# State space of a hybrid layer: strided recurrences replaced by phase rotation and real scans, by quarters

## The chip, the core and the metric

One core of a Trainium2 chip runs one program. TensorE (PE) multiplies, VectorE (DVE), ScalarE (ACT) and GpSimd (POOL) work on vectors, SyncE (SP) issues transfers. The metric is the device time of one execution in microseconds; the median of three runs is given.

## What is computed

One step of a decoder layer over 2048 prompt tokens and 8 x 8 sample tokens. The part that matters is the S5 state space: 32 groups of 16 channels, each driving 64 complex states, with a constant complex factor a per state:

```python
bu_re = einsum('blgc,gpc->blgp', ug, bb_re); bu_im = einsum('blgc,gpc->blgp', ug, bb_im)
h[t] = a * h[t-1] + bu[t]            # complex, a = exp(lam * dt)
y = einsum('blgp,gcp->blgc', h_re, c_re) - einsum('blgp,gcp->blgc', h_im, c_im)
y = gelu(y + d_skip * u); y = y * sigmoid(y @ w_glu + b_glu)
```

An RWKV-7 head group, an output projection, a ConvFFN and a final norm follow.

## The kernel before

Four functions run one after the other, each with its engines in blocks that all end before the next begins: `project_in` (RMS norm and input projection), `state_space`, `delta_rule` and `dense_tail`. The change is in `state_space` alone. All of it works in f32; a TensorE product of f32 shows as two MATMUL and two LDWEIGHTS instructions, a transpose as one of each.

Tokens are taken in blocks of L = 8, so there are NBL = 256 prompt blocks and 8 sample blocks. Partitions hold 64 states of two groups; j runs over the 16 pairs of groups (`NJ`), and the real and imaginary parts are separate tensors. The order is:

1. u (512 channels x tokens) is turned round by transposes into `U`, in three lots: two of 128 prompt blocks and one of 8 sample blocks (`LOTS`). ScalarE evicts.
2. VectorE makes the parameters: `Ap` (powers 0 to 8 of a), `CA` (C times powers), `R` (B times powers) and `Qp` (powers 8 to 128). TensorE makes the kernel rows K from `CA` and `Bb` (64 products with 64 rows each; `groups` takes groups of one parity into one bank), ScalarE evicts them to `Ks`, and eight transfers place shifted copies into `Tm`, to which VectorE adds d on the diagonal. `R` is transposed to `RT`.
3. The driving term of each block, `RT` x `U`, goes to `H`; ScalarE evicts the real part, VectorE the imaginary.
4. VectorE runs the recurrence over 256 blocks: 15 steps inside each of 16 stretches of 16 blocks (strided views of `H`), 15 steps over the ends (`G`), 16 corrections. Each is `add_product`, eight operations of 256 elements, every one waiting for the last. `h_ready` goes up after half and after all of the corrections.
5. Per lot and group TensorE sums `U` x `Tm` (128 rows), `Hr` x `CAr` and `Hi` x `CAn` (64 rows each, upper or lower half of the array by the parity of the group), ScalarE takes the gelu into `rows`, TensorE transposes back and VectorE copies into u (L2188).
6. The GLU: 96 products over tiles of 352 tokens (L2275), ScalarE's sigmoid, VectorE's product (L2191).

VectorE's operations of a chain are written through the helper `tt` (L2047), which issues one and waits for it.

## Time and profile before

| what | value |
|---|---|
| median of 3 runs | 3719.92 us (3714.68 to 3720.4) |
| profiled execution, its own time | 3721.35 us |
| its span | 3719.6 us |
| mean granted TensorE clock | 0.934 of 2.4 GHz |
| PE busy | 3323.8 us (89%) |
| DVE busy | 2210.6 us (59%) |
| ACT busy | 1165.9 us (31%) |
| POOL busy | 174.8 us (5%) |
| state space, from its first transfer to the next stage's | 482.1 to 920.0 us |

Busy shares are averages over stages that have different limits. An instruction's duration holds its way through the pipeline, so for a dense stream the distance from start to start counts, not the duration. The granted clock is given as a share of 2.4 GHz; 0.50 is 1.2 GHz.

### The profile page before, as it was taken

How to read it: one execution, taken by the hardware profiler on the slowest of the kernel's cores; microseconds unless marked ns; L12 is line 12 of the kernel's file. 1: busy time of each engine (PE TensorE's matmuls, PEld its weight loads, DVE VectorE, ACT ScalarE, POOL GpSimd, SP SyncE). 2: the span in 40 equal slices, each digit the busy share in tenths (PEclk: the TensorE clock that was granted, in tenths of full speed). 3: DMA queues.
4: the chain of work that ended last, by engine and by line, in shares of the span. 5: the costliest groups of instructions: out<-in, count | busy, mean ns of one | idle time of the engine just before them, and what ended most of it. 6: DMA issues, size and time to landing. Idle time of an engine off the chain costs nothing.

```text
span 3719.6 us, 75947 instructions
## 1 busy us (share of the span) xinstructions
PE 3323.8 (89%) x32916; PEld 3146.2 (85%) x32916; DVE 2210.6 (59%) x4339; ACT 1165.9 (31%) x2283; POOL 174.8 (5%) x178
## 2 busy tenths in 40 slices
PE   6899961298899998987889999999999999999997
PEld 6899951175678787877889999999999999999997
DVE  6655568931677777743455555565555655555555
ACT  4333330011444545432332222232222322222432
POOL 0000000000110101001210000000000000000121
PEclk8999975579899999988999999999999999999999
DMA  4443320000100100003332222222222222222222
GB/s 145 132 145 115 112 43 0 0 2 29 30 23 23 32 23 23 18 15 97 96 92 69 68 71 72 69 63 69 71 72 69 63 69 73 70 68 73 82 85 85
DMA packets 332589, 237.73 MB, mean 64 GB/s; under 512 B 16720, under 2 KB 319440, under 8 KB 332240
## 3 DMA queue, kind: packets, MB, share of 16 engines
q1 hardware_dynamic: 332256, 232.87, 21.5%
q8 instruction: 260, 4.26, 0.5%
q14 instruction: 73, 0.60, 0.1%
HBM read 206.28 MB, written 25.38 MB: 62 GB/s over the span
## 4 chain that ended last, share of the span: by engine, by line
PE 47%; DVE 3%; DMA 2%; issue 1%; ACT 1%; SPq 0%; DVEq 0%; ACTq 0%
PE tail_bank L987 27%; PE tail_bank L1024 13%; PE tail_bank L1043 5%; DMA tail_raw<-in_w_out 2%; PE tail_bank L975 2%; PE tail_bank L1056 1%; ACT tail_w_hi L634 1%; DVE tail_x L787 0%; DVE tail_xn_lo L792 0%; DVE tail_xn_lo L775 0%; DVE mix_b L799 0%; DMA tail_raw<-in_w_pg 0%; DVE mix_b L918 0%; DVE mix_a L799 0%; DMA tail_raw<-in_w_gate 0%
## 5 line engine op out<-in xcount | busy, mean ns | idle before, releaser
L987 PE MATMUL tail_bank<-tail_xn_hi,tail_w_hi 128*128 128x352 f32 x2112 | 682.4, 323 | 9.5 <-DVE tail_xn_lo L792 9.5
L987 PE MATMUL tail_bank<-tail_xn_lo,tail_w_hi 128*128 128x352 f32 x2112 | 680.5, 322 | 0.0
L987 PE MATMUL tail_bank<-tail_xn_hi,tail_w_lo 128*128 128x352 f32 x2112 | 680.5, 322 | 0.0
L987 PEld LDWEIGHTS tail_bank<-tail_xn_hi,tail_w_hi 128*128 128x128 f32 x2112 | 397.5, 188 | 13.0 <-issue 7.3
L987 PEld LDWEIGHTS tail_bank<-tail_xn_lo,tail_w_hi 128*128 128x128 f32 x2112 | 397.8, 188 | 0.1
L987 PEld LDWEIGHTS tail_bank<-tail_xn_hi,tail_w_lo 128*128 128x128 f32 x2112 | 397.7, 188 | 0.0
L1024 PE MATMUL tail_bank<-tail_f_hi,tail_wd_hi 128*128 128x352 f32 x1056 | 341.8, 324 | 7.2 <-DVE mix_b L893 2.7
L1024 PE MATMUL tail_bank<-tail_f_lo,tail_wd_hi 128*128 128x352 f32 x1056 | 339.6, 322 | 0.0
L1024 PE MATMUL tail_bank<-tail_f_hi,tail_wd_lo 128*128 128x352 f32 x1056 | 339.6, 322 | 0.0
L770 DVE TENSOR_TENSOR tail_w_lo<-tail_raw,tail_w_hi 128x1024 fp32r<-128x1024 f32 x180 | 220.6, 1226 | 165.6 <-ACT tail_w_hi L634 165.4
L634 ACT CAST tail_w_hi<-tail_raw 128x1024 fp32r<-128x1024 f32 x180 | 185.5, 1046 | 406.4 <-DMA tail_raw<-in_w_gate 210.8
L384 PE MATMUL in_pp<-in_x_hi,in_w_hi 128*128 128x352 f32 x864 | 285.7, 331 | 26.2 <-DVE in_w_lo L266 25.5
L385 PE MATMUL in_pp<-in_x_lo,in_w_hi 128*128 128x352 f32 x864 | 283.2, 328 | 0.0
L386 PE MATMUL in_pp<-in_x_hi,in_w_lo 128*128 128x352 f32 x864 | 282.9, 327 | 0.0
L856 DVE TENSOR_SCALAR tail_cv<-tail_gp,tail_cw 128x352 f32<-128x352 f32 (+1 forms) x132 | 60.7, 460 | 361.2 <-ACT tail_gp L695 184.0
L1024 PEld LDWEIGHTS tail_bank<-tail_f_hi,tail_wd_hi 128*128 128x128 f32 x1056 | 198.3, 188 | 12.9 <-DVE mix_a L893 7.1
L1024 PEld LDWEIGHTS tail_bank<-tail_f_lo,tail_wd_hi 128*128 128x128 f32 x1056 | 198.4, 188 | 0.0
L1024 PEld LDWEIGHTS tail_bank<-tail_f_hi,tail_wd_lo 128*128 128x128 f32 x1056 | 198.3, 188 | 0.0
L384 PEld LDWEIGHTS in_pp<-in_x_hi,in_w_hi 128*128 128x128 f32 x864 | 167.1, 193 | 29.1 <-DVE in_w_lo L266 14.6
L695 ACT COPY tail_gp<-tail_bank 128x352 f32<-128x352 f32 x110 | 50.0, 454 | 440.9 <-PE tail_bank L987 440.9
L2252 PE MATMUL ss_bk<-ss_Tm,ss_U 128*128 128x128 f32 (+1 forms) x192 | 53.2, 366 | 137.4 <-DVEq L2177 137.4
L385 PEld LDWEIGHTS in_pp<-in_x_lo,in_w_hi 128*128 128x128 f32 x864 | 166.9, 193 | 0.6 <-issue 0.5
(441 smaller groups left out, 6952.2 us busy)
## 6 DMA issues: line engine op xcount, KB each, us to landing
tail_raw<-in_w_gate SPq DMA_DIRECT2D x66, 512.0 KB, 4.0
tail_raw<-in_w_val SPq DMA_DIRECT2D x66, 512.0 KB, 4.0
tail_raw<-in_w_down SPq DMA_DIRECT2D x66, 512.0 KB, 3.6
in_raw<-in_w_in SPq DMA_DIRECT2D x54, 512.0 KB, 4.1
in_xs<-in_xT SPq DMA_DIRECT2D x12, 1408.0 KB, 6.8
scratch_zr<-in_zo SPq DMA_DIRECT2D x84, 176.0 KB, 1.9
rw_z<-scratch_zr SPq DMA_DIRECT2D x16, 896.0 KB, 5.6
tail_raw<-in_w_out SPq DMA_DIRECT2D x24, 512.0 KB, 4.6
```

The lines of the kernel that those rows point to most:

```text
L384: pe.matmul(out, wh[:, k, :], xh[:, k, tok(n)], start=(k == 0), stop=False)
L385: pe.matmul(out, wh[:, k, :], xl[:, k, tok(n)], start=False, stop=False)
L386: mm = pe.matmul(out, wl[:, k, :], xh[:, k, tok(n)], start=False, stop=(k == KD - 1))
L634: act.copy(as_block(weight_slot(i)[0], i), raw[i % NRAW][:]).then_inc(w_hi, 1)
L695: act.copy(gp[:, 2 + n * TW:2 + (n + 1) * TW], pg[b][:, 0:TW]).then_inc(gate_out, 1)
L770: dve.tensor_tensor(as_block(lo, i), raw[i % NRAW][:], as_block(hi, i).bitcast(F32), ALU.subtract).then_inc(w_lo, 1)
L856: end = dve.tensor_scalar(out, row(2), tap[2], tap[3], ALU.mult, ALU.add)
L975: mm = pe.matmul(pp[i % NPP][:, 0:TW], l, r, start=(k == 0 and j == 0), stop=(k == KD - 1 and j == 2))
L987: mm = pe.matmul(out[:, 0:TW], l, r, start=(k == 0 and j == 0), stop=(k == KD - 1 and j == 2))
L1024: mm = pe.matmul(pd[i % 4][:, 0:TW], l, r, start=(q == 0 and j == 0), stop=(q == G - 1 and j == 2))
L1043: mm = pe.matmul(eg[i % 3][:, 0:TW], l, r, start=(k == 0 and j == 0), stop=(k == KD - 1 and j == 2))
L2252: pe.matmul(out, U[:, g, b0:b0 + n], Tm[:, g, :], start=True, stop=False)
```

## The change

The states are handled in four quarters of four pairs j (`JC`), one per 128 channels (`ct`), with two sets of `U` and `H` in turn. The recurrence over blocks is done otherwise: with a^8 = rho * e^(i phi), the driving terms are multiplied by e^(-i phi n), after which real and imaginary parts each follow h[n] = rho h[n-1] + b[n] with a real factor. A hardware scan along the 256 blocks does that, and the result is turned back by e^(i phi n). The factors of the turn for blocks 0 to 127 (`turn_low`) are made by GpSimd in seven doublings, those of 128 to 255 (`turn_high`) by VectorE. In each quarter VectorE makes the real part of the turned driving terms and GpSimd the imaginary part (`im_ready`), two products and a difference; the scans and the turning back are VectorE's.

Beside that: u is turned round quarter by quarter (`own_rows`) through two banks, and ScalarE evicts both parts of the driving terms (`driven`) and the transposes back into u (`channels`). The block's tokens are held in reverse slots. `R` and `CA` are each made in six whole operations. d is added by GpSimd to a 16-row `Ks` ahead of the transfers rather than to `Tm` after them. In the K products and in the outputs the two parities alternate from product to product, into two banks; the eight full products of a quarter's lot come first and the sixteen half ones after. The GLU is as before, on other banks.

```diff
-        U = e.sb("U", [P, NG_, NBT])
-        H = [e.sb(n, [P, NJ, NBL + 1]) for n in ("Hr", "Hi")]
+        turn_low, turn_high = (e.sb(n, [P, 2, NJ, HALF_NB]) for n in ("turn_low", "turn_high"))
+        NU, NH = GB_ * NBT, 2 * JC * (NBL + 1)
+        own = [e.sb(f"own{i}", [P, NU + NH]) for i in range(2)]
+        U = [o[:, 0:NU].rearrange("p (g n) -> p g n", g=GB_) for o in own]
+        H = [o[:, NU:].rearrange("p (x j n) -> p x j n", x=2, j=JC) for o in own]
+        T = e.sb("T", [P, 4, JC, NBL])
...
+                sp.wait_ge(k_ready, 1)
+                sp.wait_ge(zero, 6)
                 for s in range(L):
-                    sp.dma_start(Tm[s * GC:(s + 1) * GC, :, s * GC:P], Ks[:, :, 0:P - s * GC]).then_inc(t_moved, 16)
-                sp.wait_ge(end_ready, 2)
...
+                def tt(out, a, b, op):
+                    count[0] += 1
+                    pool.tensor_tensor(out, a, b, op).then_inc(links, 1)
+                    pool.wait_ge(links, count[0])
+                pool.wait_ge(pw_ready, 1)
+                pool.wait_ge(zero, 6)
+                w = 1
+                for i in range(NW - 1):
+                    by = [bcast(x[:, i, :], w) for x in Pw]
+                    first, then = [[turn_low[:, x, :, a:a + w] for x in range(2)] for a in (0, w)]
+                    t = T[:].rearrange("p k j n -> p k (j n)")[:, 0, 0:NJ * w].rearrange("p (j n) -> p j n", n=w)
+                    tt(then[0], first[0], by[0], ALU.mult)
+                    tt(t, first[1], by[1], ALU.mult)
+                    tt(then[0], then[0], t, ALU.subtract)
+                    tt(then[1], first[0], by[1], ALU.mult)
+                    tt(t, first[1], by[0], ALU.mult)
+                    tt(then[1], then[1], t, ALU.add)
+                    w *= 2
+                pool.sem_inc(low_ready, 1)
+                pool.wait_ge(par_in, 16 * NPAR)
+                pool.wait_ge(ca_ready, 1)
+                pool.tensor_tensor(dI, ident[0:GC, 0:GC].unsqueeze(1).to_broadcast([GC, NG_, GC]), bcast(d[0:GC, :], GC), ALU.mult).then_inc(dI_ready, 1)
+                pool.wait_ge(k_out, 2 * KU)
+                pool.wait_ge(dI_ready, 1)
+                pool.tensor_tensor(Ks[:, :, 0:GC], Ks[:, :, 0:GC], dI, ALU.add).then_inc(k_ready, 1)
+                def turned(out, x, part, ct):
+                    for i, turn in enumerate((turn_low, turn_high)):
+                        at_ = slice(i * HALF_NB, (i + 1) * HALF_NB)
+                        count[0] += 1
+                        pool.tensor_tensor(out[:, :, at_], x[:, :, at_], turn[:, part, JC * ct:JC * (ct + 1), :], ALU.mult).then_inc(links, 1)
+                pool.wait_ge(high_ready, 1)
+                for ct in range(KU):
+                    pool.wait_ge(b_out, 2 * JC * (ct + 1))
+                    if ct:
+                        pool.wait_ge(h_ready, ct)
+                    h = [H[ct % 2][:, x, :, 1:] for x in range(2)]
+                    turned(T[:, 2], h[1], 0, ct)
+                    turned(T[:, 3], h[0], 1, ct)
+                    pool.wait_ge(links, count[0])
+                    pool.tensor_tensor(T[:, 2], T[:, 2], T[:, 3], ALU.subtract).then_inc(im_ready, 1)
...
+                def squared(out, a):
+                    tt(s["x1"], a[0], a[1], ALU.subtract)
+                    tt(s["x2"], a[0], a[1], ALU.add)
+                    link(dve.scalar_tensor_tensor(out[1], a[0], 2.0, a[1], ALU.mult, ALU.mult))
+                    tt(out[0], s["x1"], s["x2"], ALU.mult)
...
+                        tt(x, x, s["x2"], ALU.mult)
+                pw = [[x[:, i, :] for x in Pw] for i in range(NW)]
+                squared(pw[1], [s["cos"], s["sin"]])
+                squared(pw[2], pw[1])
+                squared(pw[0], pw[2])
+                unit(pw[0], s["rho"])
+                for i in range(1, NW):
+                    squared(pw[i], pw[i - 1])
+                    if i % 3 == 0:
...
-                tt(CA[0][:], big[0], big[1], ALU.subtract)
-                tt(big[0], at_[0], c_[1], ALU.mult)
-                tt(big[1], at_[1], c_[0], ALU.mult)
-                tt(CA[1][:], big[0], big[1], ALU.add)
-                dve.tensor_scalar(CA[1][:], CA[1][:], -1.0, None, ALU.mult).then_inc(k_ready, 1)
-                for q in range(L):
-                    a = [bcast(x[:, L - 1 - q, :], GC) for x in Ap]
-                    cmul([R[0][:, :, q, :], R[1][:, :, q, :]], a, [x[:] for x in Bb], t4)
-                dve.sem_inc(r_ready, 1)
-                for i in range(2):
-                    link(dve.tensor_copy(Qp[i][:, 1, :], Ap[i][:, L, :]))
...
-                dve.wait_ge(t_moved, 16 * L)
+                tt(CA[0][:], at_[0], c_[0], ALU.mult)
+                tt(big, at_[1], c_[1], ALU.mult)
+                tt(CA[0][:], CA[0][:], big, ALU.subtract)
...
+                dve.wait_ge(low_ready, 1)
...
-                def add_product(x, a, b, t):
...
-                def run(i):
-                    return [x[:, :, 1 + i:1 + i + BI * (BI - 1) + 1:BI] for x in H]
-                a8 = [bcast(x[:, 1, :], BI) for x in Qp]
-                for i in range(1, BI):
-                    add_product(run(i), a8, run(i - 1), t4)
...
-                    add_product([x[:, :, b] for x in G], a128, [x[:, :, b - 1] for x in G], tj)
-                for r in range(BI):
-                    blocks = [x[:, :, 1 + r * BI:1 + (r + 1) * BI] for x in H]
-                    add_product(blocks, [x[:, 1:, :].rearrange("p i j -> p j i") for x in Qp], [bcast(x[:, :, r], BI) for x in G], t4)
-                    if r % (BI // 2) == BI // 2 - 1:
-                        dve.sem_inc(h_ready, 1)
-                a8s = [bcast(x[:, 1, :], NBS) for x in Qp]
-                add_product([x[:] for x in HS], a8s, [x[:] for x in h0], [x[:, :, 0:NBS] for x in tmp])
...
+                def rotate(ct):
+                    h = [H[ct % 2][:, x, :, 1:] for x in range(2)]
+                    t = [T[:, k] for k in range(4)]
+                    def turned(out, x, part):
+                        for i, turn in enumerate((turn_low, turn_high)):
+                            at_ = slice(i * HALF_NB, (i + 1) * HALF_NB)
+                            last = dve.tensor_tensor(out[:, :, at_], x[:, :, at_], turn[:, part, JC * ct:JC * (ct + 1), :], ALU.mult)
+                        link(last)
+                    dve.wait_ge(b_out, 2 * JC * (ct + 1))
+                    turned(t[0], h[0], 0)
+                    turned(t[1], h[1], 1)
+                    tt(t[0], t[0], t[1], ALU.add)
+                    for x in range(2):
+                        if x:
+                            dve.wait_ge(im_ready, ct + 1)
+                        for jj in range(JC):
+                            j = ct * JC + jj
+                            last = dve.tensor_tensor_scan(t[2 * x + 1][:, jj, :], s["rho"][:, j:j + 1].to_broadcast([P, NBL]), t[2 * x][:, jj, :], 0.0,
+                                                          ALU.mult, ALU.add)
+                    link(last)
+                    turned(t[0], t[1], 0)
+                    turned(t[2], t[3], 1)
+                    tt(h[0], t[0], t[2], ALU.subtract)
+                    turned(t[0], t[1], 1)
+                    turned(t[2], t[3], 0)
+                    tt(h[1], t[0], t[2], ALU.add)
+                    for x in range(2):
+                        last = dve.tensor_copy(endp[x][:, JC * ct:JC * (ct + 1)], H[ct % 2][:, x, :, NBL])
+                    last.then_inc(h_ready, 1)
...
+                        j = ct * JC + jj
+                        for x in range(2):
+                            if j:
+                                pe.wait_ge(b_out, 2 * (j - 1) + x + 1)
+                            for h in range(2):
+                                last = pe.matmul(bk_b[x][NS * h:NS * h + NS, 0:NBT], RT[x][:, j, NS * h:NS * h + NS], U[ct % 2][:, 2 * jj + h, :],
+                                                 start=True, stop=True)
+                            last.then_inc(b_mm, 1)
+                def outputs(ct, lot):
+                    b0, n, _ = LOTS[lot]
+                    i0 = upto(ct) + 2 * lot
+                    if i0 >= 4:
+                        pe.wait_ge(y_out, i0 - 2)
+                    out = [[bk_y[(i0 + q) % 4][0:n, k * P:(k + 1) * P] for k in range(JC)] for q in range(2)]
+                    for q in range(2):
+                        for k in range(JC):
+                            pe.matmul(out[q][k], U[ct % 2][:, 2 * k + q, b0:b0 + n], Tm[:, GB_ * ct + 2 * k + q, :], start=(k == 0), stop=False)
+                    last = [None, None]
+                    for x in range(2):
+                        for k in range(JC):
+                            for q in range(2):
+                                h = slice(NS * q, NS * q + NS)
+                                j = ct * JC + k
+                                state = h0[x][h, j, :] if b0 == NBL else H[ct % 2][h, x, k, b0:b0 + n]
+                                last[q] = pe.matmul(out[q][k], state, CA[x][h, j, 1:, :], start=False, stop=(x == 1 and k == JC - 1))
+                    for q in range(2):
+                        last[q].then_inc(y_mm, 1)
...
+                pe.wait_ge(ca_ready, 1)
+                for c in range(KU):
+                    if c >= 2:
+                        pe.wait_ge(k_out, 2 * (c - 1))
+                    last = [None, None]
+                    for k in range(JC):
+                        for n in range(2):
+                            for q in range(2):
+                                j, h = JC * c + k, slice(NS * q, NS * q + NS)
+                                last[q] = pe.matmul(bk_y[(2 * c + q) % 4][0:GC, k * P:(k + 1) * P], Bb[n][h, j, :], CA[n][h, j, 0:L, :],
+                                                    start=(n == 0), stop=(n == 1))
+                    for q in range(2):
...
+                own_rows(1)
+                driven(1)
+                pe.wait_ge(k_out, 2 * KU)
+                pe.wait_ge(t_moved, 16 * L)
+                for ct in range(KU):
+                    pe.wait_ge(h_ready, ct + 1)
+                    outputs(ct, 0)
+                    outputs(ct, 1)
+                    channels(ct, 0)
+                    outputs(ct, 2)
+                    channels(ct, 1)
+                    channels(ct, 2)
+                    if ct + 2 < KU:
+                        own_rows(ct + 2)
+                        driven(ct + 2)
```

## Rows read from the trace of the kernel before

**Rows 1.** Busy us (and instructions) of PE, PEld, DVE, ACT, POOL per stretch; PEclk, DMA share, GB/s.
```profile
482.10:541.90 59.80, 44.83 (x320) 36.94 (x320) 48.44 (x107) 28.70 (x62) 3.60 (x3) 0.67 0.11 31
...
585.30:722.00 136.70, 0.00 (x0) 0.00 (x0) 125.94 (x308) 0.66 (x1) 0.00 (x0) 0.52 0.00 0
722.00:782.30 60.30, 60.02 (x192) 45.59 (x192) 34.82 (x74) 4.38 (x8) 0.00 (x0) 0.50 0.01 3
782.30:788.80 6.50, 6.05 (x33) 6.05 (x34) 4.90 (x6) 0.39 (x1) 0.00 (x0) 0.58 0.00 0
788.80:822.50 33.70, 33.70 (x193) 25.89 (x192) 2.71 (x3) 4.18 (x7) 0.00 (x0) 1.00 0.00 1
822.50:858.60 36.10, 33.72 (x257) 17.15 (x256) 9.24 (x16) 6.57 (x10) 0.00 (x0) 1.00 0.00 1
858.60:919.90 61.30, 58.76 (x192) 37.24 (x192) 9.82 (x7) 13.27 (x24) 0.00 (x0) 0.97 0.00 1
```

**Rows 2.** Waits, 480 to 921 us: us in total, times, longest.
```profile
PE ss_bk L2252 <- DVEq L2177: 137.4, 1, 137.4
```

**Rows 3.** DVE groups by form in the state space: busy us, mean ns, idle before.
```profile
L2047 DVE TENSOR_TENSOR ss_Hr<-ss_Hr,ss_tmp 128x256 f32<-128x256 f32 x62 | 31.2, 504 | 2.1
...
L2047 DVE TENSOR_TENSOR ss_CAr<-ss_Hr,ss_Hi 128x2304 f32<-128x2304 f32 x1 | 2.6, 2557 | 0.0
```

**Rows 4.** Timeline of DVE after sine and cosine: start us, us.
```profile
492.48 0.18 DVE L2047 TENSOR_TENSOR ss_Apr<-ss_mag,ss_cos 128x16 f32<-128x16 f32 x1 [0.44 <-ACT ss_cos L2004]
492.69 0.17 DVE L2047 TENSOR_TENSOR ss_Api<-ss_mag,ss_sin 128x16 f32<-128x16 f32 x1
```

**Rows 5.** DVE groups by form in the delta rule, 925 to 1650 us.
```profile
L1432 DVE TENSOR_TENSOR rw_yt<-rw_yt,rw_bonus_h 128x512 f32<-128x512 f32 x16 | 11.1, 692 | 0.5
...
L1313 DVE TENSOR_TENSOR_SCAN rw_p_L<-rw_seg,rw_p_w 128x256 f32<-128x256 f32 x1 | 0.7, 692 | 0.0
```

**Rows 6.** POOL groups by form, whole span.
```profile
L1267 POOL TENSOR_TENSOR rw_p_t<-rw_p_t,rw_r_k 128x512 f32<-128x512 f32 x16 | 16.6, 1038 | 1.3
...
L1267 POOL TENSOR_TENSOR rw_p_t<-rw_p_t,rw_r_k 128x256 f32<-128x256 f32 x1 | 0.6, 612 | 0.1
```

**Rows 7.** Timeline of DVE and POOL in the delta rule.
```profile
1126.50 1.23 DVE L1313 TENSOR_TENSOR_SCAN rw_p_L<-rw_seg,rw_p_w 128x512 f32<-128x512 f32 x1
1126.60 1.65 POOL L1256 TENSOR_TENSOR rw_rT<-rw_z,rw_p_E 128x256 f32<-128x256 f32 x1 [17.91 <-DVE rw_p_w L1311]
...
1127.64 1.15 DVE L1318 TENSOR_TENSOR rw_p_t<-rw_p_a,rw_kah 128x512 f32<-128x512 f32 x1
```

**Rows 8.** Timeline of PE in the K products, clock 0.50; entries that overlap are merged.
```profile
522.26 0.63 PE L2222 MATMUL ss_bk<-ss_CAn,ss_Bbi 64*16 64x128 f32 x2
522.68 0.63 PE L2222 MATMUL ss_bk<-ss_CAr,ss_Bbr 64*16 64x128 f32 x4
523.09 0.65 PE L2222 MATMUL ss_bk<-ss_CAn,ss_Bbi 64*16 64x128 f32 x4
```

**Rows 9.** Timeline of SP's queue and DVE around the transfers into Tm.
```profile
542.16 13.90 SPq L1968 DMA_DIRECT2D ss_Tm<-ss_Hi  x8
...
558.63 4.42 DVE L2047 TENSOR_TENSOR ss_Hr<-ss_ident,ss_d 128x4096 f32<-128x4096 f32 x1 [9.05 <-DMA ss_Tm<-ss_Hi]
```

**Rows 10.** Timeline of PE in the driving terms, clock 1.00.
```profile
573.32 0.62 PE L2240 MATMUL ss_bk<-ss_U,ss_RTi 128*64 128x264 f32 x4
...
573.77 0.62 PE L2240 MATMUL ss_bk<-ss_U,ss_RTr 128*64 128x264 f32 x4
```

**Rows 11.** Timeline of PE in the outputs of the sample lot, clock 1.00.
```profile
829.27 0.39 PE L2252 MATMUL ss_bk<-ss_Tm,ss_U 128*8 128x128 f32 x2
...
830.11 0.39 PE L2252 MATMUL ss_bk<-ss_Tm,ss_U 128*8 128x128 f32 x2
```

**Rows 12.** ACT groups by form in the state space.
```profile
L1994 ACT COPY ss_rows<-ss_bk 128x512 f32<-128x512 f32 x16 | 8.1, 671 | 0.0
...
L2018 ACT COPY ss_Hr<-ss_bk 128x256 f32<-128x256 f32 x16 | 6.0, 372 | 29.4 <-PE ss_bk L2240 29.4
```

More of the change, by code:

```diff
@@ L1922, in state_space @@
[L1922 to L1925 removed]
+        dI = B[0:GC].rearrange("p x j c -> p (x j) c")
+        big = own[1][:, 0:NJ * (L + 1) * GC].rearrange("p (j t c) -> p j t c", t=L + 1, c=GC)
@@ L1943, in state_space, with u_turn, x_turn, upto @@
         LOTS = [(0, P, 0), (P, P, P * L), (NBL, NBS, SEQ)]
-        NK = NG_ // 4
+        NLOT = len(LOTS)
         NR = 2 * NJ // 4
-        UF, UG = KU * 2, NG_ // 4
-        UL = UF + UG
-        def groups(i):
-            first = 8 * (i // 2) + i % 2
-            return slice(first, first + 7, 2)
+        UT, XT = 4 * NLOT, 2 * NLOT
+        def u_turn(ct, lot, f):
+            return ct * UT + lot * 4 + f + max(ct - 1, 0) * XT
+        def x_turn(ct, lot, half):
+            return (min(ct, KU - 2) + 2) * UT + ct * XT + lot * 2 + half
+        def upto(ct):
+            return 2 * NLOT * ct
+        def halves(x, ct):
+            return [x[:, i, JC * ct:JC * (ct + 1), :] for i in range(2)]
         with nc.Block() as block:
@@ new lines, in _, with powers @@
+                cmul([x[:] for x in Bb], [bcast(s["fr"], GC), bcast(s["fi"], GC)], [Br, Bi], st)
+                n = 1
+                while n < L:
+                    last = [x[:, n:n + 1, :].to_broadcast([P, n, NJ]) for x in Ap]
+                    t = small_t[:, 0:n * NJ].rearrange("p (i j) -> p i j", j=NJ)
+                    cmul([x[:, n + 1:2 * n + 1, :] for x in Ap], [x[:, 1:1 + n, :] for x in Ap], last, t)
+                    n *= 2
+                def powers(first, count_):
+                    return [x[:, first:first + count_, :].rearrange("p t j -> p j t").unsqueeze(3).to_broadcast([P, NJ, count_, GC]) for x in Ap]
@@ new lines, in _ @@
+                tt(big, at_[1], c_[0], ALU.mult)
+                link(dve.scalar_tensor_tensor(CA[1][:], CA[1][:], -1.0, big, ALU.mult, ALU.subtract))
+                link(dve.memset(H[1][:, :, :, 0:1], 0.0))
+                dve.sem_inc(ca_ready, 1)
+                dve.wait_ge(low_ready, 1)
+                dve.wait_ge(r_mm, NR)
+                for j in range(0, NJ, NJ // 2):
+                    js = slice(j, j + NJ // 2)
+                    by = [bcast(x[:, NW - 1, js], HALF_NB) for x in Pw]
+                    t = T[:, 0].rearrange("p j n -> p (j n)").rearrange("p (j n) -> p j n", n=HALF_NB)
+                    cmul([turn_high[:, x, js, :] for x in range(2)], [turn_low[:, x, js, :] for x in range(2)], by, t)
@@ new lines, in channels @@
+                def channels(ct, lot):
+                    _, n, _ = LOTS[lot]
+                    pe.wait_ge(y_out, upto(ct) + 2 * lot + 2)
+                    for half in range(2):
+                        i = x_turn(ct, lot, half)
+                        pe.wait_ge(t_out, i - 1)
+                        for k in range(4):
+                            c = (4 * half + k) * P
+                            last = pe.transpose(bk_t[i % 2][:, k * n:(k + 1) * n], yrow[lot][0:n, c:c + P], ident[0:n, 0:n])
+                        last.then_inc(t_mm, 1)
@@ L2224, in _ @@
+                own_rows(0)
                 pe.wait_ge(r_ready, 1)
```

340 lines of the change are left out of this document (157 added, 183 removed).

## The prediction

> **What bounds the kernel now.** I read the page first, then the busy time by stretches, then the waits inside the state space. The four stages follow one another with a barrier between them, so time saved in one comes off the end as long as the next does not change. The page gives 3719.6 us of span, and the state space holds 482.1 to about 920 of it. The reader is to see three things in [rows 1]. VectorE works alone for 136.7 us (585.3 to 722.0, TensorE 0.00 busy). The output products then take 60.3 us for the first lot and 33.7 us for the second, though both have 192 instructions: the granted clock is 0.50 (1.2 GHz) in one and 1.00 (2.4 GHz) in the other. Last come the third lot and its transposes (36.1 us) and the GLU (61.3 us), which is TensorE's. [Rows 2] names the big wait: TensorE waits 137.4 us for VectorE's recurrence. The diff touches nothing outside `state_space`, so I take 482.1 us ahead of the stage and 2799.7 us behind 919.9 as they are.
>
> **Prices.** VectorE, contiguous f32 pair operations: 512 elements 0.692, 2304 elements 2.557 us [rows 3, 5], so 1.04 ns an element plus 0.16 us; linked small ones start every 0.21 us [rows 4]. So 256 cost 0.43, 1024 cost 1.23, 2048 cost 2.29, each plus 0.03 for the link. A scan of 256 takes 0.692 us [rows 5], about 0.61 in a run of four, since the next starts under the end of the last. GpSimd: 256 elements 0.612, 512 1.038 us [rows 6], so 1.66 ns an element plus 0.19 us.
>
> **The start.** From the first operation after sine and cosine (492.5, [rows 4]) VectorE now does 59 small operations for the powers of the turn (12.4 us), 4 for rho and 15 for `Ap` and f (4.0), `Bb` 6 x 0.46 = 2.8, powers of `Ap` 18 x 0.26 = 4.6, `R` in six whole operations 6 x 2.32 = 13.9, `CA` 6 x 2.59 = 15.5. That ends at 545.9. `turn_high` is 12 x 1.26 = 15.1 more: 561.0 if nothing disturbs it.
>
> GpSimd makes `turn_low` beside that: 42 operations over 6 x (16 + ... + 1024) = 12192 elements, 20.3 us of elements and 42 x 0.27 of fixed cost, some 32 us from 505. Whether it is beside or instead is what [rows 7] shows: a GpSimd product of 256 elements takes 1.65 us where it meets a VectorE scan with two SBUF inputs, against 0.612 alone, and VectorE's next product of 512 elements takes 1.15 instead of 0.692. They take turns. I charge 15 of the 20.3 us to VectorE, since its small operations are mostly fixed cost; the bounds are 0 and 20. So `ca_ready` is at 561 and the turns are whole at 576.
>
> The Trainium skill (SBUF — State Buffer, "Who interferes with whom") says the same as a rule: a VectorE instruction with two SBUF inputs and a GpSimd instruction that reads SBUF exclude each other for the whole instruction. By that rule the whole 20.3 us of doubling and the 5.1 us of each rotation would be added to VectorE's own; the upper bounds here.
>
> The K products, 64 of them: [rows 8] shows how two 64-row products share the array: four entries apart by 0.42 us hold 2 instructions while they are in one half, and 4 each where the halves change (522.68 and 523.09). The new order changes the half at every product, so 64 x 0.213 = 13.7 us at 1.2 GHz: 561 to 574.7. GpSimd adds d to `Ks` (1.5 us with the eviction). The eight copies into `Tm` before ran from 542.16 until VectorE, which waited for them, started at 558.63 [rows 9]: 16.5 us, so 576.2 + 16.5 = 592.7. On SyncE only the stores of the states stand behind them, whose end the GLU covers. On GpSimd the imaginary parts of all quarters are queued behind this addition: a K product later than 576 would hold the first rotation too. The two VectorE operations on `Tm` (4.42 us each, [rows 9] has the first) go.
>
> **One rotation.** VectorE: two turned products (2.8), a sum (1.3), four scans (2.5), four scans for the imaginary part (2.5), four turned products (5.4), two sums (2.6), copies (0.4) = 17.4 us. GpSimd: 4 x 512 + 1024 = 3072 elements = 5.1 us, which by [rows 7] delays VectorE by the same. 22.6 us, between 17.4 (free) and 26 (dearer GpSimd operations); all on VectorE it would be 21.5. Four of them are 90 us. They replace 46 times `add_product`, eight operations each, at up to 504 ns on average for 256 strided elements [rows 3]: 136.7 us in the open and 35 more under the first outputs [rows 1]. The first is ready at 576 + 22.6 = 598.6, 6 us behind `Tm`. GpSimd starts each one only when VectorE has ended the last (they share `T`), so it never works ahead; that costs nothing as long as they take turns anyway.
>
> **TensorE becomes the bound after that.** Before, three products (128, 64 and 64 rows) took 33.7 / 32 = 1.05 us at full clock, 60.3 / 32 = 1.88 at half [rows 1]. Now a lot of a quarter is 8 full products x 0.32 + 0.2 = 2.8 us and 16 half products in pairs. Columns in pairs overlap fully: 64-column products of 264, two to an item, take 0.45 us an item [rows 10], half of 2 x 4 x 264 / 2.4 GHz. For row pairs I take 0.16 us each; bounds 0.107 (loading hidden) and 0.32 (no pairs). So 5.4 us a lot at 2.4 GHz, 10.6 at 1.2. The sample lot takes 0.84 us for three before [rows 11]; in the new order 8 x 0.21 + 16 x 0.107 + 0.2 = 3.6. The transposes back are 4 us a quarter; their copies into u move from VectorE to ScalarE (0.67 each by [rows 12]), as do the imaginary driving terms. Turning u round for the next quarter passes two banks to and fro: 8 copies of 0.67 and 4 smaller ones taken at 0.4 (7 us), and 8 pairs of 0.37 + 0.17 (4.3, [rows 4, 12]), with the waits for one another 16 us. Gelu and copies make 17 us of ScalarE in a quarter, under TensorE's 34.
>
> The clock: dense outputs stayed at 0.50 for 60.3 us and only 32 transposes raised it (0.58 on average in that stretch, 1.00 after) [rows 1]. In the new order transposes come every quarter and pauses are short, so I charge half clock for two lots of the first quarter only.
>
> Quarter 0: 598.6 + 2 x 10.6 + 3.6 + 4 = 627.4; the next u and its products to 643.4. The third rotation needs these and ends at 666, covered. Quarter 1: 18.4 to 661.8; u of quarter 3 to 677.8. Quarter 2 to 696.2; the fourth rotation runs 677.8 to 700.4 and is late by 4. Quarter 3 to 718.8. GLU starts there, not at 858.6: **139.8 us less**. The GLU's 61.3 us stand [rows 1]. Of the profiled execution's 3719.6 us span 3579.8 remain (its own time is 1.8 us more, the median of the runs 0.3 more). I say **3580**.
>
> **The rivals.** (A) *The clock stays at 1.2 GHz through the outputs.* Six more lots at +5.2, three sample lots at +3.6: 42 us, 3622. For it: 60 us of dense products did not raise it. Against: transposes did, within 6.5 us. 17%. (B) *GpSimd is free beside VectorE.* The first rotation ends at 561.0 + 17.4 = 578.4, `Tm` is there at 577.7, so the start is 20 us earlier, and the fourth rotation is covered (4 us): 3556. Against: [rows 7]. 13%. (C) *No row pairs in the outputs,* each half product 0.32: 8 lots x 2.6 + 4 x 1.7 and drains between full and half products: 3610. Against: [rows 8]. 10%. 8-column products alone would be 3 x 0.213 = 0.64 us and take 0.84 [rows 11], so each group pays 0.2 for going from full to half height and back. The Trainium skill (TensorEngine Tiling (Array Packing), "Key Properties") states that changing the tiling mode drains the array; the trace agrees with its 0.2 us. (D) *Slower: GpSimd prices.* If its operations, with their broadcasts, short inner runs and links, cost more than 7.4 ns an element instead of 1.66, the 12192 + 12288 elements add over 140 us and the gain is gone; at 8 ns it is 3735. The dearest row is 1.65 us for 256, 6.4 ns, and most of that is waiting. 2%. (E) That offloading the imaginary part does nothing is in my own sum: 22.6 against 21.5 us a quarter. My forecast has 58%, its own range 3560 to 3600.
>
> **Range and chances.** Low end: B and loading of weights half hidden (0.13 instead of 0.16, some 4 us) on top, a little more for the handing to and fro: 3545. High end: A with 5 us more lock and 10 us dearer rotations, 3635. A change of 0.2%, 7 us, is about what a measurement of this kernel can tell from none; all cases but D are far beyond it. Faster 0.97, same 0.01, slower 0.02.
>
> **What would show it.** Turned products on VectorE at about 1.1 to 1.4 us instead of 0.69 in the first third of each rotation, and GpSimd products over 1.04, show the turns taken; equal to the rows of before, B. `Tm` copies ending some 6 us ahead of the first rotation. A granted clock of 1.00 in quarters 1 to 3, else A. Two instructions of half products in 0.16 us or less each, else C. GLU starting near 719. The forecast is wrong above all if TensorE waits for VectorE in each quarter, or if the handing to and fro of two banks costs far more than 16 us.

## The result and the profile after

The changed kernel takes 3572.62 us (median of four runs, 3572.05 to 3573.4) against 3720.14 for the kernel before beside it: a ratio of 0.9607, 95% interval 0.959 to 0.9624. That is 147.5 us less, where 139.8 was forecast; 3580 was said and 3572.6 came.

The profiled execution took 3572.05 us with a span of 3570.3. Its stages, by the same columns as [rows 1]:

```profile
482.00:582.00 100.00, 33.15 (x280) 24.93 (x280) 86.49 (x140) 25.56 (x59) 60.02 (x50) 0.65 0.10 22
582.00:605.00 23.00, 5.40 (x43) 2.38 (x41) 22.60 (x26) 6.01 (x21) 8.74 (x6) 0.75 0.23 36
605.00:624.00 19.00, 17.34 (x170) 15.34 (x171) 18.76 (x20) 7.34 (x12) 9.37 (x5) 0.85 0.01 1
624.00:641.00 17.00, 14.15 (x84) 8.91 (x83) 3.08 (x6) 9.71 (x29) 0.00 (x0) 0.70 0.00 1
641.00:713.00 72.00, 56.94 (x582) 46.80 (x580) 46.64 (x58) 31.23 (x64) 19.38 (x10) 0.91 0.01 3
713.00:774.00 61.00, 58.77 (x194) 37.34 (x192) 9.74 (x6) 14.78 (x26) 0.00 (x0) 0.97 0.00 1
```

Up to 582 VectorE (third column of busy time) is the bound, as it was before, but the 136.7 us of the recurrence have shrunk to the 23 us of one rotation. From 605 TensorE's own chain sets the pace; it waits for two rotations and, while it turns u, for ScalarE's copies (14.15 of 17.0 us busy between 624 and 641). The GLU (last line) is what it was in [rows 1]; it starts at 713.0 instead of 858.6, which is 145.6 us of the 149.3 by which the span shrank. The other 3.7 lie in stages that the change does not touch. In the runs below the start of the state space alone moves between 479.7 and 483.8 us with the same code ahead of it, so 3.7 is no result.

The waits of the stage (480 to 780 us: in total, times, longest), the answer to [rows 2]:

```profile
PE ss_bk L2349 <- DVE ss_endi L2293: 23.3, 2, 16.3
DVE ss_T L2271 <- ACT ss_HSi L2081: 22.5, 2, 13.9
```

TensorE waits twice for a rotation, 16.3 us for the first and 7.0 for the last, where it waited 137.4. The second line is the reverse: VectorE waits 13.9 and 8.6 us for the driving terms of the third and fourth quarter.

VectorE and GpSimd at the end of the start, then in the first rotation (timeline: start us, us):

```profile
560.06 4.58 DVE L2248 SCALAR_TENSOR_TENSOR ss_CAn<-ss_CAn,ss_own 128x2304 f32<-128x2304 f32 x1
...
582.05 1.72 DVE L2271 TENSOR_TENSOR ss_T<-ss_own,ss_turn_low 128x512 f32<-128x512 f32 x1
...
588.59 3.25 DVE L2141 TENSOR_TENSOR ss_T<-ss_T 128x1024 f32<-128x1024 f32 x1
591.87 4.77 DVE L2283 TENSOR_TENSOR_SCAN ss_T<-ss_rho,ss_T 128x256 f32<-128x256 f32 x8
596.67 0.69 DVE L2271 TENSOR_TENSOR ss_T<-ss_T,ss_turn_low 128x512 f32<-128x512 f32 x1
...
604.65 0.69 DVE L2271 TENSOR_TENSOR ss_T<-ss_own,ss_turn_low 128x512 f32<-128x512 f32 x1
```
```profile
557.68 4.53 POOL L2005 TENSOR_TENSOR ss_turn_low<-ss_turn_low,ss_T 128x1024 f32<-128x1024 f32 x1
...
583.18 1.63 POOL L2036 TENSOR_TENSOR ss_T<-ss_own,ss_turn_high 128x512 f32<-128x512 f32 x1
```

While GpSimd works, VectorE's operation of 2304 elements takes 4.58 us (2.557 in [rows 3]), its 512 elements 1.7 (0.692 in [rows 5]), its 1024 elements 3.25; when GpSimd is done, the same 512 take 0.69. GpSimd's 1.63 for 512 are dearer than the 1.038 of [rows 6] as well. From the first turned product (582.05) to that of the next rotation (604.65) it is 22.6 us.

TensorE in the first outputs, and at full clock in those of the second quarter (x16 is 8 products):

```profile
604.89 3.75 PE L2349 MATMUL ss_bk<-ss_Tm,ss_own 128*128 128x128 f32 x16 [16.29 <-DVE ss_endi L2293]
608.57 2.08 PE L2357 MATMUL ss_bk<-ss_CAr,ss_own 64*128 64x128 f32 x16
610.44 1.15 PE L2357 MATMUL ss_bk<-ss_CAn,ss_own 64*128 64x128 f32 x16
611.53 2.05 PE L2349 MATMUL ss_bk<-ss_Tm,ss_own 128*128 128x128 f32 x16
...
640.47 2.05 PE L2349 MATMUL ss_bk<-ss_Tm,ss_own 128*128 128x128 f32 x16
642.45 1.16 PE L2357 MATMUL ss_bk<-ss_CAr,ss_own 64*128 64x128 f32 x16
643.45 1.06 PE L2357 MATMUL ss_bk<-ss_CAn,ss_own 64*128 64x128 f32 x16
644.43 0.82 PE L2349 MATMUL ss_bk<-ss_Tm,ss_own 128*128 128x128 f32 x5
```

From start to start, eight full products take 1.98 us and eight half ones 1.00: a lot takes 4.0 us. At 1.2 GHz (first two lines) the same are 3.7 and 1.9. The change from one to the other comes at 610.6, 5.7 us into the outputs (the granted clock is 0.50 up to 610.4, 0.70 over 610.4 to 610.8, then 1.00); [rows 1] show 60 us at 0.50 for the same products in another order.

### The profile page after: what moved, and what is told of

Same layout as the page of the kernel before. It is cut to its first block, busy times and chain, and to the rows that moved or that the text cites. A ratio compares the mean times of both kernels' runs of the same rounds, so it can differ in the third digit from the quotient of the medians.

```text
span 3570.3 us, 75777 instructions
## 1 busy us (share of the span) xinstructions
PE 3247.9 (91%) x32916; PEld 3095.3 (87%) x32916; DVE 2139.0 (60%) x4012; ACT 1190.6 (33%) x2339; POOL 268.4 (8%) x245
## 4 chain that ended last, share of the span: by engine, by line
PE 47%; DVE 3%; issue 3%; DMA 3%; ACT 1%; POOL 0%; SPq 0%; DVEq 0%; POOLq 0%; ACTq 0%
PE tail_bank L987 28%; PE tail_bank L1024 13%; PE tail_bank L1043 3%; DMA tail_raw<-in_w_out 2%; PE tail_bank L975 2%; PE tail_bank L1056 1%; ACT tail_w_hi L634 1%; DVE tail_x L787 0%; DVE tail_xn_lo L792 0%; DVE tail_xn_lo L775 0%; DVE mix_b L799 0%; POOL tail_ssum L625 0%; DMA tail_raw<-in_w_pg 0%; DVE mix_a L799 0%; DVE mix_b L918 0%
## 5 line engine op out<-in xcount | busy, mean ns | idle before, releaser
L386 PEld LDWEIGHTS in_pp<-in_x_hi,in_w_lo 128*128 128x128 f32 x864 | 165.9, 192 | 0.0
```

Source lines behind the costliest of these rows:

```text
L386: mm = pe.matmul(out, wl[:, k, :], xh[:, k, tok(n)], start=False, stop=(k == KD - 1))
```

## The experiments

Besides the time, two places of the profile are compared: the end of the first rotation and the start of the GLU, both counted from the moment at which GpSimd's first wait of the stage ends, because the stages ahead shift by some us from run to run. For the changed kernel these are the rows (waits of GpSimd; timeline of TensorE):

```profile
POOL ss_Apr L1995 <- POOLq L125: 481.5, 1, 481.5
```
```profile
713.02 58.75 PE L2421 MATMUL ss_bk<-mix_a,ss_wglu 128*128 128x352 f32 x192
```

So 231.5 for it (713.02 - 481.5); in e1_im_vector the two are 483.8 and 709.22, and 225.4 the difference. The last two columns come from one execution of each kernel, the profiled one, which took 3563.7 us in e7_all, 3558.1 in e9_turn_first and 3647.9 in e4_old_order, 5 to 8 us more than their medians. All of them:

| kernel | median us | ratio to before, 95% | first rotation over | GLU starts |
|---|---|---|---|---|
| changed | 3572.6 | 0.9607 (0.959 to 0.9624) | 123.2 | 231.5 |
| e1_im_vector | 3567.5 | 0.9583 (0.9569 to 0.9597) | 121.1 | 225.4 |
| e2_low_vector | 3571.2 | 0.9594 (0.958 to 0.9608) | 125.1 | 231.2 |
| e3_apart | 3592.6 | 0.9652 (0.9635 to 0.9668) | 123.1 | 249.3 |
| e4_old_order | 3642.8 | 0.9788 (0.9773 to 0.9803) | 123.3 | 308.0 |
| e5_split | 3563.9 | 0.9582 (0.9569 to 0.9595) | 118.0 | 221.2 |
| e6_early | 3566.3 | 0.9588 (0.9575 to 0.9601) | 123.1 | 226.5 |
| e7_all | 3555.4 | 0.9561 (0.9547 to 0.9575) | 117.7 | 218.1 |
| e8_warm | 3550.9 | 0.9541 (0.9528 to 0.9554) | 117.8 | 209.0 |
| e9_turn_first | 3553.4 | 0.9549 (0.9536 to 0.9562) | 117.7 | 216.8 |

The time spent at 1.2 GHz behind a rotation is not the same in each of these executions, though the products and their order are. In the changed kernel, e1_im_vector, e2_low_vector and e5_split it was 5.7, 4.4, 2.9 and 3.5 us in the first quarter and 4.6, 3.0, 3.5 and 3.5 in the fourth (from the first output to the rise of the granted clock). With what the clock does while u is turned, that moves the start of the GLU by 2 to 3 us, so a smaller difference in the last column is no result.

### e1_im_vector: the imaginary part on VectorE

```diff
 # gpsimd
-                    turned(T[:, 2], h[1], 0, ct)
-                    turned(T[:, 3], h[0], 1, ct)
...
-                    pool.tensor_tensor(T[:, 2], T[:, 2], T[:, 3], ALU.subtract).then_inc(im_ready, 1)
 # vector
+                    turned(t[2], h[1], 0)
+                    turned(t[3], h[0], 1)
+                    tt(t[2], t[2], t[3], ALU.subtract)
...
-                            dve.wait_ge(im_ready, ct + 1)
```

> The imaginary part of the turned driving terms is made by VectorE, in line with the rest; GpSimd has no part in the rotations. Theory (GpSimd and VectorE take turns, so the handing over only adds GpSimd's dearer operations): a rotation takes 21.5 us by the contiguous VectorE prices instead of 22.6. Rotations 0 and 3 are the ones that the end waits for, so 1 to 3 us less than the changed kernel's 3572.6: about 3571. Rival (GpSimd works for nothing beside VectorE): the rotation grows by 4.1 us, on two rotations 8 us: about 3581.

Measured: 3567.5 us, 5.1 less than the changed kernel in the medians, where 1 to 3 were expected; the two intervals overlap a little, but the trace is plain. The first rotation, its five operations for the imaginary part (588.11 to 592.03) and the start of the second (timeline of VectorE):

```profile
584.19 0.69 DVE L2253 TENSOR_TENSOR ss_T<-ss_own,ss_turn_low 128x512 f32<-128x512 f32 x1
...
588.11 0.69 DVE L2253 TENSOR_TENSOR ss_T<-ss_own,ss_turn_low 128x512 f32<-128x512 f32 x1
...
592.03 4.77 DVE L2266 TENSOR_TENSOR_SCAN ss_T<-ss_rho,ss_T 128x256 f32<-128x256 f32 x8
...
604.81 0.68 DVE L2253 TENSOR_TENSOR ss_T<-ss_own,ss_turn_low 128x512 f32<-128x512 f32 x1
```

A rotation takes 20.6 us (604.81 - 584.19) and not 22.6. GpSimd's help costs 2.0 us a rotation, nearly twice the 1.1 of the prediction's point E. The rival, that it works for nothing, falls. The GLU starts 6.1 us sooner: two rotations make 4.0 of that, and the rest is the shorter time at 1.2 GHz in the first and fourth quarter.

### e2_low_vector: the doublings on VectorE

```diff
-                dve.wait_ge(low_ready, 1)
+                w = 1
+                for i in range(0, NW - 1):
+                    by = [bcast(x[:, i, :], w) for x in Pw]
+                    first, then = [[turn_low[:, x, :, a:a + w] for x in range(2)] for a in (0, w)]
...
+                    cmul(then, first, by, t)
+                    w *= 2
```

The same operations go out of GpSimd's part.

> All seven doublings of turn_low go to VectorE, in the place where it now waits for them; GpSimd does nothing there. Theory (take turns): VectorE's whole operations CA and R fall back to 2.56 and 2.29 us, the convolution's coefficients are ready at about 546 us instead of 564.7, the 42 operations cost VectorE 20.7 us (12.7 us of elements, 8 us of fixed cost), and the turns are whole at 581.7 us where they now are at 581.9: the time stays at 3572.6 within 2 us. Rival (the doublings on GpSimd cost VectorE nothing, its operations are long for another reason): 20.7 us more, about 3593.

Measured: 3571.2 us, as the theory has it. With GpSimd at rest VectorE's `CA` is back at its own price:

```profile
528.90 2.56 DVE L2126 TENSOR_TENSOR ss_CAr<-ss_Apr,ss_Cr 128x2304 f32<-128x2304 f32 x1
...
544.50 0.07 DVE L2234 MEMSET ss_own<- 128x8 f32 x1
544.71 0.18 DVE L2126 TENSOR_TENSOR ss_turn_low<-ss_turn_low,ss_Pwr 128x16 f32<-128x16 f32 x1
...
582.46 1.72 DVE L2262 TENSOR_TENSOR ss_T<-ss_own,ss_turn_low 128x512 f32<-128x512 f32 x1
```

Counted from the stage's start `CA` is whole 18.7 us sooner (544.5 - 480.0 against 564.7 - 481.5). The doublings on VectorE then take 22.5 us, of which 1.7 are two meetings with GpSimd's small additions, and the turns are whole 1.9 us later than in the changed kernel. So GpSimd takes 20.8 us of work off VectorE (22.5 less the two meetings) and costs it 18.7 in lengthened operations. In the changed kernel the two small additions meet operations of `turn_high` instead, for 1.9 us (2.12 and 2.17 us where the others take 1.22).

### e3_apart: the half products of one half of the array after those of the other

```diff
-                    for x in range(2):
-                        for k in range(JC):
-                            for q in range(2):
+                    for q in range(2):
+                        for x in range(2):
+                            for k in range(JC):
```

> The output products of a lot keep full height first and half height after, but all half-height products of one half of the array run before those of the other, so that neighbours never lie in different halves. Theory (neighbours in different halves run two at a time, which is where 0.125 us per half-height product at full clock comes from): each takes 0.25 to 0.32 us instead, 2 to 3 us more in each of eight lots and 1 to 2 in the four sample lots, 20 to 28 us in all: about 3597. Rival (their order does not matter, only the switch between full and half height does): no change, 3573.

Measured: 3592.6 us, 20.0 more, at the low end of what was expected, but by another sum. Outputs of the second quarter at full clock (x8 is 4 products):

```profile
649.70 2.05 PE L2349 MATMUL ss_bk<-ss_Tm,ss_own 128*128 128x128 f32 x16
651.68 1.16 PE L2357 MATMUL ss_bk<-ss_CAr,ss_own 64*128 64x128 f32 x8
652.67 0.72 PE L2357 MATMUL ss_bk<-ss_CAn,ss_own 64*128 64x128 f32 x5
...
655.10 2.05 PE L2349 MATMUL ss_bk<-ss_Tm,ss_own 128*128 128x128 f32 x16
```

The full products are unchanged (1.98); four half products now take the 0.99 us that eight took: 0.25 instead of 0.125 each. The lot takes 5.4 us, 1.4 more, where 2 to 3 were expected: the middle of it, at the step from one half to the other, still overlaps. A sample lot takes 1.3 more (5.0 us, 661.53 to 666.54). The first two lots took 20.3 us at 0.50 throughout, and 10.6 (604.89 to 615.50) in the changed kernel: 9.7 more, most of it clock. By quarters, each from its first output to the next one's (the last to the GLU), the run takes 9.7, 4.9, 0.0 and 3.4 us more, and the GLU starts 17.8 later. The third quarter's dearer products cost nothing, because TensorE's wait for the fourth rotation behind them shrank from 7.0 to 3.1 us; the second quarter also makes part of its driving terms at 1.2 GHz, for 1 us more. The first two lots as a window (columns as above):

```profile
604.40:624.70 20.30, 20.25 (x96) 19.40 (x96) 20.02 (x22) 1.79 (x3) 9.47 (x5) 0.50 0.00 1
```

### e4_old_order: the order of the kernel before

```diff
...
                     for q in range(2):
                         for k in range(JC):
                             pe.matmul(out[q][k], U[ct % 2][:, 2 * k + q, b0:b0 + n], Tm[:, GB_ * ct + 2 * k + q, :], start=(k == 0), stop=False)
-                    for x in range(2):
-                        for k in range(JC):
-                            for q in range(2):
...
+                            for x in range(2):
```

> The output products of a lot go back to the order of the kernel before: for each item and block full height, real half, imaginary half. Theory: each group of three costs 1.05 us at full clock and 1.88 at half, as in the rows of before, so a lot takes 8.4 or 15 us where it now takes 4.0 or 7.5; eight lots add 35 to 60 us, the sample lots 4 x 3 us: 3615 to 3640; and the granted clock stays at 0.50 for longer in the first quarter than now. Rival (the order is worth nothing and the gain over before's products comes from less waiting): 3573.

Measured: 3642.8 us, 70 more (just above the 3640 at the end of what was expected), nearly half of what the whole change gained. At full clock the group of three costs what it cost before (670.52 to 671.58), and in the first quarter the clock stays at 0.50 for 66 us of outputs, turning and driving terms, up to 669.7:

```profile
670.52 0.49 PE L2350 MATMUL ss_bk<-ss_Tm,ss_own 128*128 128x128 f32 x2
...
671.58 0.49 PE L2350 MATMUL ss_bk<-ss_Tm,ss_own 128*128 128x128 f32 x2
```
```profile
603.50:633.50 30.00, 29.93 (x96) 22.79 (x96) 21.99 (x25) 1.79 (x3) 9.46 (x5) 0.50 0.00 1
633.50:667.00 33.50, 30.25 (x137) 17.17 (x136) 0.00 (x0) 13.33 (x26) 0.00 (x0) 0.50 0.00 0
667.00:730.00 63.00, 58.61 (x364) 39.97 (x360) 38.15 (x41) 21.53 (x55) 19.32 (x10) 0.95 0.00 1
...
743.00:770.00 27.00, 27.00 (x88) 20.49 (x88) 0.00 (x0) 1.79 (x3) 0.00 (x0) 0.50 0.00 1
```

The last line is from the fourth quarter, which is at 0.50 from 741.5 until the GLU starts at 788.1. No wait for VectorE stands before it: its rotation was over at 736.4, and TensorE came to it from the small transposes of `channels`, before which it waited 0.82 and 0.45 us for ScalarE:

```profile
739.88 0.38 PE L2367 MATMUL ss_bk<-ss_ident,ss_late 8*128 8x8 f32 x4 [0.82 <-ACT mix_a L2097]
740.70 0.41 PE L2367 MATMUL ss_bk<-ss_ident,ss_late 8*128 8x8 f32 x4 [0.45 <-ACT mix_a L2097]
741.04 0.49 PE L2350 MATMUL ss_bk<-ss_Tm,ss_own 128*128 128x128 f32 x2
```

So the order carries two things. One is 1.05 against 0.50 us a group: by the 0.25 us of a half product without a partner in e3_apart a group would take 0.75, so 0.25 are the lost pairing and 0.3 the going between full and half height in every group (the 0.2 of the prediction's rival C). The other is how long 1.2 GHz lasts once it is there: 3 to 6 us or 46 and 66. What took the clock down at 741.5, after so short a wait, was not tried.

### e5_split: GpSimd only where VectorE's operations are small

```diff
-                for i in range(NW - 1):    # gpsimd
+                for i in range(4):
+                for i in range(4, NW - 1): # vector, after CA, by cmul
```

and the imaginary part on VectorE as in e1_im_vector.

> GpSimd makes only the doublings of 1 to 8 steps, whose operations fall beside small operations of VectorE; VectorE makes the last three doublings (18 operations of 256, 512 and 1024 elements) after CA, and the imaginary part of the driving terms. Theory (take turns): CA and R take their own 2.56 and 2.29 us, 18 operations cost 6 x (0.46 + 0.72 + 1.26) = 14.6 us, where the lock now costs 20.9 us, and GpSimd's long ones stop: turns whole at about 576 us instead of 581.9, first rotation over at about 597 instead of 604.65; 8 us less, about 3565. Rival (GpSimd's long doublings were mostly free): 10 us more, about 3583.

Measured: 3563.9 us, 8.7 less, as expected, though some 3 us of the 10.3 by which the GLU starts sooner are time at 1.2 GHz. The first rotation is over 5.2 us sooner (7 to 8 expected): `CA` takes 2.56 us an operation, but the last three doublings come to 16.3 us for my 14.6, by two meetings with GpSimd's additions again (1.16 and 2.17 us instead of 0.42 and 1.22). The four small doublings are a gain on GpSimd: `CA` is whole 54.0 us after sine and cosine, and 53.1 in e2_low_vector with GpSimd at rest. So they cost VectorE 0.9 us, where its own making of them took 6.2 in e2_low_vector.

### e6_early and e7_all: full products ahead of the wait

```diff
-                    pe.wait_ge(h_ready, ct + 1)
-                    outputs(ct, 0)
-                    outputs(ct, 1)
+                    full(ct, 0)
+                    full(ct, 1)
+                    pe.wait_ge(h_ready, ct + 1)
+                    half_products(ct, 0)
+                    half_products(ct, 1)
...
-                    outputs(ct, 2)
+                    full(ct, 2)
+                    half_products(ct, 2)
```

> In each quarter the full-height products of lots 0 and 1 (triangle times driving terms), which need no rotated state, are issued before TensorE waits for the rotation. Theory: in the first quarter 16 of them lie in TensorE's wait of 16 us (7.4 us at half clock), as long as the triangle is in its place by 593 us; in the fourth they lie in the wait of 7 us (4 us at full clock); the other two quarters have no wait to fill. 7 to 11 us less, about 3564. If the granted clock rises sooner for it, another 2 us. Rival (the triangle comes too late, or the clock falls back to half while TensorE waits on): 0 to 3 us less, 3571.

> The divided doublings with the imaginary part on VectorE, and the full-height products ahead of the wait, together. Theory: the first rotation ends 8 us sooner, which makes the wait of TensorE only 8 to 9 us longer than its 7.4 us of early products: gains add up if the triangle is there by 589 us: 15 to 18 us less, about 3556. Rival (the transfers of the triangle end near 593 us and are then what sets the start): 8 to 12 us less, about 3562.

Measured: 3566.3 and 3555.4 us, 6.3 and 17.2 less, where 7 to 11 and 15 to 18 were expected. In e6_early (timeline of TensorE, then a stretch):

```profile
590.68 5.44 PE L2349 MATMUL ss_bk<-ss_Tm,ss_own 128*128 128x128 f32 x32 [3.59 <-DMA ss_Tm<-ss_late]
603.49 2.08 PE L2362 MATMUL ss_bk<-ss_CAr,ss_own 64*128 64x128 f32 x16 [7.36 <-DVE ss_endi L2293]
```
```profile
618.00:637.00 19.00, 16.39 (x82) 10.19 (x82) 7.65 (x12) 9.49 (x28) 0.00 (x0) 0.55 0.00 1
```

`Tm` is there at 590.7, before anything needs it. The full products leave the path, but behind them the turning of u and the driving terms run at a mean clock of 0.55, for 18.8 us (617.99 to 636.82) where the changed kernel took 16.8 (623.68 to 640.47); in the second quarter they take 16.6 where it took 15.0. Without these 3.6 us the GLU would start 8.6 us sooner and not 5.0. The half-height products behind the wait still begin at 1.2 GHz, for 5.3 us. In e7_all `Tm` comes at 576.1, since the K products follow `CA`; that rival falls.

### e8_warm and e9_turn_first: the clock behind the wait

```diff
+                    for i in range(5 if ct == 0 else 0):
+                        full(ct, 0, again=True)
+                        full(ct, 1, again=True)
                     full(ct, 0)
                     full(ct, 1)
```

In e9_turn_first `own_rows(ct + 2)` and `driven(ct + 2)` also come before the three `channels`, on TensorE and ScalarE.

> As the version with the divided doublings and the early full-height products; in the first quarter TensorE makes these full-height products six times over instead of once (each time anew, so the numbers are the same), which fills its wait of 20.9 us for the first rotation with 19 us of work at full clock. Theory (the half clock behind the wait comes from the wait): the half-height products of lots 0 and 1 start at 2.4 GHz and take 4 us instead of 6.1, and the turning of the input rows behind them (two transposes of 1.94 at half clock in each of its parts) keeps full clock more of the time: 2 to 7 us less than the version without repeats (3555), about 3550. Rival (what the clock does behind the wait hangs on the products that come then): no change, or up to 4 us more where the repeats end after the rotation.

> As the one with the repeats; in each quarter TensorE and ScalarE turn the input rows of the quarter after next and make its driving terms before they turn the quarter's outputs back, instead of after. Theory (the rotations of the third and fourth quarter wait for these driving terms, and TensorE waits for the fourth rotation): rotations start 3 to 5 us sooner, but TensorE's wait for the fourth rotation is down to about 2 us there, so 1 to 3 us less than the run with the repeats alone. Rival (TensorE's own work is the bound from the first output on, and the order of it is worth nothing): the same time; the turning back then comes just before the next quarter's products and its copies may delay them by up to 3 us.

Measured: 3550.9 and 3553.4 us; about 3550 was expected for the first, and 1 to 3 us less than it for the second. The half-height products after the rotation, in e7_all first, then in e8_warm:

```profile
600.81 2.08 PE L2352 MATMUL ss_bk<-ss_CAr,ss_own 64*128 64x128 f32 x16 [20.88 <-DVE ss_endi L2283]
602.68 1.92 PE L2352 MATMUL ss_bk<-ss_CAn,ss_own 64*128 64x128 f32 x16
```
```profile
600.11 1.16 PE L2352 MATMUL ss_bk<-ss_CAr,ss_own 64*128 64x128 f32 x16 [1.40 <-DVE ss_endi L2283]
601.11 1.06 PE L2352 MATMUL ss_bk<-ss_CAn,ss_own 64*128 64x128 f32 x16
```

Work that is thrown away buys 2.4 GHz for what follows: from its first half-height product to the next quarter's outputs the first quarter takes 27.0 us (600.11 to 627.14) where it took 33.2 in e7_all (600.81 to 634.04). What that is worth at the end is less sure. In the profiled executions the GLU starts 9 us sooner, but 3 of them lie in the second quarter, long after the repeats. In the medians 4.5 us are left, and the executions overlap (3551.1 to 3563.7 without, 3547.4 to 3552.5 with), as do the two intervals.

Turning u first makes the third rotation start 4.0 us sooner and the fourth 1.4, but the time is the same or 2.5 us worse. The small transposes of `channels` with their waits for ScalarE now stand right ahead of the next quarter's products, and these begin at 1.2 GHz. Sixteen full products (x32) take 6.63, 5.38 and 6.42 us in the second to fourth quarter, and 3.84 in e8_warm; the second quarter's, in e8_warm first, then in e9_turn_first:

```profile
627.14 3.84 PE L2339 MATMUL ss_bk<-ss_Tm,ss_own 128*128 128x128 f32 x32
```
```profile
625.71 6.63 PE L2338 MATMUL ss_bk<-ss_Tm,ss_own 128*128 128x128 f32 x32
```

So a shorter wait on VectorE gained nothing there. In e4_old_order too the clock fell right behind these small transposes; that they are the cause is read from the traces and was not tried by itself.

## Why the prediction was right

The table has the forecast's own steps (us) beside what the trace of the changed kernel shows.

| step | forecast | measured |
|---|---|---|
| turns whole | 576 | 581.9 |
| one rotation | 22.6 | 22.6 (22.4 to 22.6) |
| first outputs start | 598.6 | 604.9 |
| quarter 0 until the next u's driving terms are made | 44.8 | 35.6 |
| quarter 1 | 34.4 | 31.1 |
| quarter 2, with the wait for the fourth rotation | 22.6 | 23.2 |
| quarter 3 | 18.4 | 18.2 |
| GLU starts | 718.8 | 713.0 |

- **What becomes of the recurrence**: as forecast. 136.7 us in the open became one rotation, and TensorE is the bound after that.
- **Taking turns**: right, and the term was mis-sized. 15 us were charged for the doublings; by e2_low_vector they cost 18.7. Another 1.9 came from GpSimd's two small additions, which had no term in the sum. GpSimd's own 42 operations ran for 57 us (505.3 to 562.2) and not for 32; 12 of them, with 9216 of the 12192 elements, fell beside the long operations of `R` and `CA`. The Trainium skill (SBUF — State Buffer, "Who interferes with whom") has the two exclude each other for the whole instruction; the runs agree, with 2.56 against 4.0 to 4.6 us for the same operation.
- **One rotation**: 22.6 us was forecast and 22.6 came, but by two errors of 0.7 to 0.8 that cancel, which is luck. In e1_im_vector a rotation takes 20.6 us with 3.9 for the imaginary part, so VectorE's own share is 16.7 us and not 17.4; GpSimd then adds 5.9 and not the 5.1 of its elements alone. Its operations by [rows 6], with their fixed cost, come to 6.0, so the 5.1 was not the upper bound that the prediction calls it.
- **Outputs**: the mechanism was right and the terms too high. Half products take 0.125 us, not 0.16, and full ones 0.25, not 0.32, so a lot takes 4.0 and not 5.4 us. e3_apart shows that the first figure is the pairing of neighbours in different halves. Rival C is out. The two lots of the first quarter took 10.6 us and not 21.2, 6.3 of it by these prices and 4.3 by the clock.
- **The clock**: half clock was charged for two whole lots. It lasted 5.7 us at the start, came back in the turning of u (0.52 over 625 to 635) and for 4.6 us of the last quarter, which were not charged. Rival A is out. But the reason given against it, that transposes raised the clock, is not borne out: here the clock rose among the outputs and fell among the transposes of u, and in e4_old_order it stayed at 0.50 through all transposes of the first quarter and rose in the driving terms behind them.
- **K and `Tm`**: the 64 products took 9.4 us (564.9 to 574.3), not 13.7, because the clock rose during them (0.52 over 560 to 570, then 1.00). Hidden as forecast, by a rotation that ended 13 us later than `Tm` was there, where 6 was forecast (e6_early has `Tm` at 590.7, in a stage that began 1.2 us sooner).
- **Handing u to and fro**: 16.8 us in quarter 0, and 15.0 in quarter 1 (656.58 to 671.61); 16 was said.
- **B and D** are out: GpSimd is not free, and its doublings took 4.7 ns an element with all fixed cost and waiting (57 us for 12192), where a mean of 7.4 would have been needed.

The errors offset each other in part: 6 us too few at the start, 12 too many in the first two quarters. The mechanism stands, but that the end came within 8 us is in part luck.

What the phase rotation is worth by itself was not run. The order of the output products carries 70 of the 147.5 us (e4_old_order), and if the two simply add, the 77 that are left belong to the rotation together with the work in quarters, the whole operations for `R` and `CA`, the order of the K products and d on `Ks`.

## What to carry to other kernels

GpSimd's work was largely paid for by VectorE here. Beside small operations it was a gain (the first four doublings cost VectorE 0.9 us instead of 6.2), beside long ones a loss; the last three doublings and the imaginary part moved to VectorE were worth 9 us. Let products of 64 rows alternate between the halves of the array and stand together, apart from full-height ones: the order alone was worth 70 us here. And fill TensorE's waits, first with products that need not wait (with the above 17 us), then, where the time behind the wait is TensorE's, perhaps with repeats (4.5 more in the medians, not clear of the spread): 3550.9 us against the changed kernel's 3572.6 and the 3720 of before.

## What the runs showed of the hardware

- How long 1.2 GHz lasts behind the first rotation went with the order of the products: 2.9 to 5.7 us with the halves alternating (four kernels), 22.6 us with them apart (e3_apart, 604.4 to 627.0), 66 us with full and half height mixed (e4_old_order, 603.5 to 669.7). TensorE was busy for 20.25 of the 20.3 us of outputs in the second and 29.93 of 30 in the third, so gaps in the outputs are not what kept it there. What in the stream the clock answers to was not separated.
- 19 us of repeats at full clock (e8_warm) kept it at 2.4 GHz through the outputs, but it fell again in the turning of u, whose transposes wait for ScalarE (0.74 over 615 to 620).
- GpSimd pays for the taking of turns too: 512 elements 1.63 us beside VectorE's products of 512, 2.97 to 3.18 beside its operations of 2048 elements, 1.04 alone.
- The prices of both engines come near to a sum where they meet: VectorE's 2304 elements took 4.0 to 4.6 us beside GpSimd's 1024, and 2.56 and 1.89 are the two alone (the second an estimate from the two sizes of [rows 6]).
